# The sample chunk of the delta rule, with four heads stacked on 128 partitions

## The reference, cut to what matters

```python
def step(s, xs):                      # one chunk; s is (values, keys) per head
    u = w_v_c - einsum('bhtk,bhvk->bhtv', w_k_c, s)
    o = einsum('bhtk,bhvk->bhtv', q_dec_c, s) + einsum('bhts,bhsv->bhtv', p_c, u)
    s = gl[..., None, None] * s + einsum('bhtv,bhtk->bhvk', u, k_dec_c)
    return s, o
```

## Time and profile before

| | us |
|---|---|
| runs | 2828.75, 2826.97, 2824.72 |
| median | 2826.97 |
| profiled execution | 2828.19 |
| its span, first to last instruction | 2826.6 |
| TensorE busy (share) | 2722.1 (96%) |
| VectorE busy | 1281.5 (45%) |
| ScalarE busy | 858.5 (30%) |
| GpSimd busy | 408.3 (14%) |
| mean granted TensorE clock | 0.970 |

### The profile page before, as it was taken

How to read it: one execution, slowest core, us unless ns; L and a number is a source line. 1 busy time by engine, 2 the same in 40 slices (tenths; PEclk the granted TensorE clock), 3 DMA queues, 4 the chain that set the end, 5 groups by cost and what they waited for, 6 DMA issues and landing times.

```text
span 2826.6 us, 52279 instructions
## 1 busy us (share of the span) xinstructions
PE 2722.1 (96%) x20734; PEld 2547.0 (90%) x20734; DVE 1281.5 (45%) x2130; ACT 858.5 (30%) x1429; POOL 408.3 (14%) x577
## 2 busy tenths in 40 slices
PE   7999999999888999999999999899999899999998
PEld 6999998876445899999899999899999868999998
DVE  5444227455443544432544432676445544544423
ACT  3222223234332422222422222443323223322222
POOL 3000003001442100000100000554244220100001
PEclk9999999999999999999999999999899958999999
DMA  3323322223996233332232332233101023223331
GB/s 115 89 84 92 99 75 76 61 69 112 352 341 200 60 89 89 87 104 78 60 89 83 91 103 74 58 90 82 35 1 31 9 67 98 74 83 89 99 92 43
DMA packets 404839, 263.03 MB, mean 93 GB/s; under 512 B 10954, under 2 KB 378775, under 8 KB 404665
## 3 DMA queue, kind: packets, MB, share of 16 engines
q1 hardware_dynamic: 394332, 227.22, 27.4%
q0 software_dynamic: 10384, 34.09, 3.5%
HBM read 251.71 MB, written 9.56 MB: 92 GB/s over the span
## 4 chain that ended last, share of the span: by engine, by line
PE 90%; DVE 5%; issue 1%; ACT 1%; POOL 1%; DMA 1%; SPq 0%; DVEq 0%; POOLq 0%; ACTq 0%
PE ps L484 66%; PE ps L470 5%; PE ps L2205 2%; PE ps L2226 1%; PE ps L1361 1%; PE ps L2223 1%; PE ps L1373 1%; PE ps L1413 1%; PE ps L498 1%; PE ps L1304 1%; PE ps L1322 1%; PE ps L2335 1%; PE ps L2314 1%; PE ps L1305 1%; PE ps L2189 1%
## 5 line engine op out<-in xcount | busy, mean ns | idle before, releaser
L462 DVE TENSOR_TENSOR w_lo<-w_raw,w_hi 128x1024 fp32r<-128x1024 f32 (+1 forms) x314 | 419.0, 1335 | 964.9 <-ACT w_hi L455 963.6
L484 PE MATMUL ps<-hd_hi,w_hi 128*128 128x272 f32 x3728 | 777.9, 290 | 4.0 <-DVE w_lo L462 4.0
L484 PE MATMUL ps<-hd_lo,w_hi 128*128 128x272 f32 x3728 | 771.4, 288 | 0.0
L484 PE MATMUL ps<-hd_hi,w_lo 128*128 128x272 f32 x3728 | 769.4, 288 | 0.0
L455 ACT CAST w_hi<-w_raw 128x1024 fp32r<-128x1024 f32 (+1 forms) x314 | 350.7, 1117 | 1092.9 <-PE ps L484 1031.3
L484 PEld LDWEIGHTS ps<-hd_hi,w_hi 128*128 128x128 f32 x3728 | 585.3, 189 | 12.1 <-issue 11.7
L484 PEld LDWEIGHTS ps<-hd_lo,w_hi 128*128 128x128 f32 x3728 | 587.8, 189 | 0.0
L484 PEld LDWEIGHTS ps<-hd_hi,w_lo 128*128 128x128 f32 x3728 | 584.7, 189 | 0.0
L959 POOL TENSOR_TENSOR xT<-xT,rstd_rows 128x272 f32<-128x272 f32 x96 | 81.8, 879 | 1778.5 <-DVE rstd_rows L984 1778.5
L484 PE MATMUL ps<-h_hi,w_hi 128*128 128x272 f32 x1232 | 255.0, 288 | 0.0
L484 PE MATMUL ps<-h_lo,w_hi 128*128 128x272 f32 x1232 | 254.5, 288 | 0.0
(11 more groups left out here) (493 smaller groups left out, 3230.8 us busy)
## 6 DMA issues: line engine op xcount, KB each, us to landing
w_raw<-in_ffn_w_gate_dram SPq DMA_DIRECT2D x88, 512.0 KB, 3.9
w_raw<-in_ffn_w_up_dram SPq DMA_DIRECT2D x88, 512.0 KB, 3.8
w_raw<-in_ffn_w_down_dram SPq DMA_DIRECT2D x64, 704.0 KB, 4.5
k_pages<-in_cache_a_k_dram SPq DMA_DIRECT2D x128, 256.0 KB, 4.5
v_pages<-in_cache_a_v_dram POOLq DMA_DIRECT2D x128, 256.0 KB, 4.5
w_raw<-in_c_w_in_dram SPq DMA_DIRECT2D x33, 512.0 KB, 4.1
w_raw<-in_ab_w_in_dram SPq DMA_DIRECT2D x25, 512.0 KB, 4.0
w_raw<-in_ab_w_out_dram SPq DMA_DIRECT2D x8, 512.0 KB, 3.8
```

The lines of the kernel that those rows point to most:

```text
L462: e.tensor_tensor(w_lo[:, n % 2, 0:nk * P], raw[:, n % RAW, 0:nk * P], w_hi[:, n % 2, 0:nk * P].bitcast(F32), ALU.subtract).then_inc(sem(" ...
L484: mm = e.matmul(ps[:, bank + h, 0:TH], w, x[:, k0 + k, half(h)], start=first and k == 0 and w is wh and x is x_hi, stop=last and k == nk - ...
```

## The change

The sample chunk now treats the four heads of a group as one block: 4 heads x 32 tokens = 128 partitions. Masks, decays, norms, the triangular system, right side, updates and outputs are one 128x128 tile per group where there were four 32x32 or 32x128 ones, and `incl_s`, `same_s` have 128 rows.

Products by the states are turned around. The turned states are the moving operand (128 columns), and the stationary operand is a copy of the keys or queries of one head (32 columns) that has only the tokens of sample b, all others zero. Each head writes its own 32 PSUM partitions (column groups), and the eight samples add up in one bank. GpSimd makes the masked copies in prompt chunk 3, behind the masks of levels 2 to 5. States are turned by sample, four heads into one bank, in 16 units; ScalarE copies out 12 of them, VectorE 4.

State changes are four sets (group, half of the samples) of four products with 32 rows, each head on its own rows of the array (row groups) and into its own bank. Set 0 stands between the halves of the first `c_out` unit, sets 1 to 3 ahead of units 1 to 3; VectorE's additions go between its weight splits. GpSimd masks the keys (two instructions) and issues the stores of the states.

```diff
+        def samples_masked(gp, y):                              # pool_delta
+                to = kq_m[gp][y]
+                mark(e, "pool_small", e.memset(to[:, :, :], 0.0))
...
+                e.tensor_copy(to[:, :, 0:252].rearrange("p j (b x) -> p j b x", x=36)[:, :, :, 0:DEC_S], src[:, :, 0:7, :])
+                ins = e.tensor_copy(to[:, :, 252:256], src[:, :, 7, :])
...
                     if l == 2:
                         masked_gates(c + 1)
+                    if 2 <= l < 6 and c == PT - 1:
+                        for y in range(2):
+                            samples_masked((l - 2) // 2, 2 * (l % 2) + y)
...
+            def keys_by_states(u):                              # pe_delta
...
                 for j in range(GH):
+                    mm = e.matmul(ps[j * NS:(j + 1) * NS, 4 * gp + 2, 0:P], kq_m[gp][j // 2][:, j % 2, b * NS:(b + 1) * NS],
+                                  s_turned[:, u % 8, j, :], start=b == 0, stop=b == DEC_B - 1)
...
+            def state_changes(n):
...
+                for j in range(GH):
+                    at = slice(j * NS, (j + 1) * NS)
+                    mm = e.matmul(ps[:, 4 + j, :], tile("u_vec", PT, gp)[at, 0, :],
+                                  kd_m[gp][at, 4 * q:4 * q + 4, :].rearrange("p b k -> p (b k)"), start=True, stop=True)
                 mm.then_inc(sem("ds_psum"), 1)
...
+            for u in range(2, 8):                               # TensorE's order
+                states_turned_in(u)
+                keys_by_states(u - 2)
+                if u == 3:
+                    both(corrections, PT, 1)
+                if u == 5:
+                    both(output_turned, PT - 1)
+            for u in (6, 7):
+                states_turned_in(u + 2)
+                keys_by_states(u)
+            for u in range(8):
+                queries_by_states(u)
+            for u in range(10, 16):
+                states_turned_in(u)
+                keys_by_states(u - 2)
+                if u == 10:
+                    updates(PT, 0)
+                if u == 12:
+                    outputs_within(PT, 0)
+            for u in (14, 15):
+                keys_by_states(u)
+            for u in range(8, 16):
+                queries_by_states(u)
+            updates(PT, 1)
+            outputs_within(PT, 1)
+            out_opening()                                       # unit 0 of c_out, first half of the tokens
+            state_changes(0)
             both(output_turned, PT)
...
+            outputs_out(PT, 0)                                  # VectorE's order
+            dve_split(e, gemms["c_out"]["n0"], 0, KD)
+            e.wait_ge(sem("final_state"), 2)
+            prompt_low(0)
+            prompt_low(1)
+            state_out(13)
+            for k in range(2, 5):
+                prompt_low(k)
+            right_side(PT, 1)
+            prompt_low(5)
+            outputs_out(PT, 1)
+            prompt_low(6)
+            prompt_low(7)
+            outputs_normed(PT)
+            gated(PT)
...
+            new_states(0)
```

More of the change, by code:

```diff
@@ L737, in whole @@
                     e.wait_ge(sem("y_squared"), i * per + (y_base[g["name"]] + t - 1))
[L738 to L740 removed]
+                if g["name"] == "c_out" and isinstance(i, int) and i == 0:
+                    if j == 0:
+                        e.wait_ge(sem("mixed_parts"), KD + 1)
+                        for k in range(KD):
+                            mm = pe_passes(e, n, k, x_hi, x_lo, k, 0, 1, k == 0, k == KD - 1)
+                        mm.then_inc(sem("unit_done"), 1)
+                        return
+                    state_changes(j)
                 pe_unit(e, n, i, g["nk"], x_hi, x_lo, (j % 2) * KU if per == 2 else 0, 2 * (t % 2),
[L742 to L743 removed]
+                        opens, per == 4 or j % 2 == 1)
             for j in range(4):
@@ L2182, in key_rows @@
                 e.wait_ge(sem("e_ready"), turn_of(c, gp))
-                for j in range(GH):
+                for j in range(heads(c)):
                     mm = e.transpose(bank(3, c, gp)(j), of_chunk(1, c)(gp, j), ident[:, :])
@@ L2187, in by_keys @@
             def by_keys(x, to, c, gp):
-                for j in range(GH):
-                    mm = e.matmul(bank(to, c, gp, n_of(c))(j), of_chunk(1, c)(gp, j), of_chunk(x, c)(gp, j), start=True, stop=True)
+                for j in range(heads(c)):
+                    mm = e.matmul(bank(to, c, gp)(j), of_chunk(1, c)(gp, j), of_chunk(x, c)(gp, j), start=True, stop=True)
                 mm.then_inc(sem("kk_psum"), 1)
@@ L2193, in x0 @@
                 e.wait_ge(sem("xt1_ready"), turn_of(c, gp))
-                for j in range(GH):
-                    mm = e.transpose(bank(1, c, gp, n_of(c))(j), tile("x_t", c, gp)[:, j, :], ident_of(c))
+                for j in range(heads(c)):
+                    mm = e.transpose(bank(1, c, gp)(j), tile("x_t", c, gp)[:, j, :], ident[:, :])
                 mm.then_inc(sem("x0_psum"), 1)
@@ L2339, in pe_delta, with out_opening @@
+            def out_opening():
+                g = gemms["c_out"]
+                e.wait_ge(sem("w_lo_ready"), g["first"] + 1)
+                for k in range(KD):
+                    e.wait_ge(sem("mixed_parts"), k + 1)
+                    pe_passes(e, g["first"], k, hd_hi, hd_lo, k, 0, 0, k == 0, k == KD - 1)
             both = lambda f, *args: [f(*args, gp) for gp in range(2)]
@@ L2392, in pe_delta @@
             states_turned_in(0)
+            states_turned_in(1)
             for gp in range(2):
@@ L2440, in pe_c @@
                 e.transpose(ps[:, 0, c * P:(c + 1) * P], ba_t[:, c * P:(c + 1) * P], ident[:, :])
-            e.transpose(ps[0:NS, 1, 0:P], ba_t[:, SEQ:T], ident[:, :]).then_inc(sem("tensor_stage"), reached("ba_psum"))
+            for j in range(GH):
+                mm = e.matmul(ps[j * NS:(j + 1) * NS, 1, 0:P], ba_t[:, SEQ:T], ident[:, :], start=True, stop=True)
+            mm.then_inc(sem("tensor_stage"), reached("ba_psum"))
             e.wait_ge(sem("conv_acc"), PRIMED + 24)
@@ new lines, in outputs_normed @@
+                own, n = slice(head_cols(c, 0).start, head_cols(c, 1).stop), 2 * heads(c)
+                total, root, tmp, fac = (t[:, 0:n] for t in (o_sum, o_rs, o_tmp, o_fac))
+                chain(e, e.tensor_tensor(total, total, q_sq[:, own], ALU.mult))
+                chain(e, e.tensor_scalar(total, total, EPS, None, ALU.add))
+                dve_rsqrt(e, root, tmp, total)
+                chain(e, e.tensor_tensor(fac, root, r_q[:, own], ALU.mult))
+                for gp in range(2):
+                    e.tensor_tensor(tile("o", c, gp), tile("o", c, gp), of_heads(fac[:, gp * heads(c):(gp + 1) * heads(c)], P),
```

572 lines of the change are left out of this document (265 added, 307 removed).

## The result

In the first comparison the changed kernel took **2784.6 us** (2782.4 to 2786.8, 4 runs), the kernel before 2827.0 (4 runs): ratio 0.9843 [0.9831, 0.9855], 42 us less. Predicted were 2793 us, 34 less, with a forecast range of 2781 to 2806. A second comparison on another occasion gave 2787.6 and 2827.6: 0.9855 [0.984, 0.987], 40 less. The profiled execution of after has a span of 2785.2 us, that of before 2826.6.

The account below looks back on a forecast made before the run. TensorE's list was taken to bound the kernel: 45 us gained before c_out, less 7.4 paid back, less 4.5 in chunk 3, plus 1.0, gave 34 us and 2793 us. Forecast range 2781 to 2806, whole range 2775 to 2813.

Parts of the forecast that it names:

- 1, products by the states: Before c_out: 32 sets of four key or query products, 0.35 us a set, 11.2 us at full clock.
- 2, transposes: Before c_out: 64 state transposes, eight in 0.93 us at full clock, 7.4 us instead of 13.6.
- 1 to 3 together: TensorE's products by states, transposes and small 128-partition products before c_out: 22.9 us at full clock.
- 4 and 5, waits and clock: Before c_out: waits of 12 us (6 to 18), and 8 us (0 to 22.9) for work at half speed.
- (b): TensorE's wait for the outputs of the last prompt chunk, while GpSimd scales states: 2.97 us becomes 4.6.
- (c): TensorE can't turn unit 15 until VectorE copies unit 13, behind a weight split and two low parts: 4.4 us.
- 6, state changes among units: Among c_out units: a set of four row-group products takes 1.0 us; with waits 7.4 us paid back (3.7 to 18).
- Rival B: Little gained: row groups run in turn (+10.8), clock stays 0.50 up to c_out (+15); 8 us, 2819; chance 0.11.
- 7, GpSimd in chunk 3: GpSimd's masked copies in chunk 3 hold up VectorE's norm chain, TensorE waits: 4.5 us lost (0 to 6).
- 8, smaller edits: Fewer chunk 3 transposes and square sums gain 1.0 us; constants done during the projection and moved stores cost nothing.
- A: More gained: clock holds, copy of unit 13 in time, GpSimd run leaves chain alone; 51 us, 2776; chance 0.10.
- C: Slower: with 128 columns the column groups don't overlap, 32 sets 58 us, not 11; 2840; chance 0.04 shared with another rival.

Follow-up runs that it names:

- columns_serial: Changed kernel with all four heads' products of keys and queries by the states on one group of 32 output columns: 2801.3 us.
- experiment 4: The changed kernel again, 2787.6 us, and beside it four_edits, 2772.1 us; the wait of 0.56 us is from four_edits.
- the repeat: The changed kernel measured once more, unaltered, as the base of a later batch: 2787.6 us.
- rows_serial: Changed kernel with all four products of a set of state changes reading partitions 0 to 31, one row group: 2793.2 us.
- copies_later: Changed kernel with GpSimd's masked copies between the masks of levels 3 to 6 of chunk 3, not 2 to 5: 2787.4 us.
- six_edits: four_edits plus VectorE copying state unit 5 ahead of chunk 3's gate and GpSimd's last four state scalings behind the eight low parts of c_out: 2773.4 us.
- four_edits: Changed kernel with masks built behind the c_qkv units, masked copies after the sample gates' scaling, unit 13 and right side earlier, state scaling after the norm chain: 2772.1 us.
- unit13_first: Changed kernel with VectorE's copy of state unit 13 ahead of the first weight split of c_out, not behind it and two low parts: 2785.2 us.

## Why the prediction was right, and where it was off

The mechanism was right: TensorE's list was what the end waited for, and it gave 53 us where I said 45, paid back 5.4 where I said 7.4. That the total came near also has luck in it: the miss in chunk 3 (+3) and the one in the constants (-3) cancel, and neither was foreseen. By its steps:

*1, products by the states: right.* 0.35 and 0.23 a set against 0.35; 9.3 us at full clock against 11.2. columns_serial shows that this rests on the four groups.

*2, transposes: 15% low.* Four turns between two column sets take 0.53 to 0.59 (2259.48 to 2260.07), not 0.46: about 9 us instead of 7.4. The Trainium skill, page "TensorEngine Tiling (Array Packing)", section "Key Properties", says that a change of tiling mode drains the engine; the extra 0.07 to 0.13 us per alternation is of that kind, and no run here isolates it.

*1 to 3 together: right.* 35.0 less the idles (3.27 + 0.30 + 3.08 + 0.46 = 7.1) and less half speed (5.9 x 0.49 + 6.7 x 0.38 = 5.4) leaves 22.5; I said 22.9.

*4 and 5, waits and clock: places right, sizes too large.* 7.1 against 12 and 5.4 against 8. (a) 0.30, not 2: the copies keep up. (b) 3.27, not 4.6. (c) 3.08, not 4.4. (d) 0.46, not 1. In (b) the chain stood beside GpSimd's scalings for four steps, as I had it (0.53 to 0.98 us each), and with no scaling beside it the wait was 0.56 (experiment 4). These 7.5 us are most of the surplus before c_out. That the clock came back because the work is dense in columns was argued and isn't tested: behind the same 3.27 us it stayed at half speed for 5.5 us in the trace after and for some 3.5 in the repeat.

*6, state changes among units: right.* A set takes 1.07 (1.0 forecast; the estimate of 1.2 beside it was too high), and rows_serial shows 3.7 without row groups. The waits are 0.45, 1.47 and 0.34. What I left out: c_out now opens at full clock, where before its opening ran at 0.50, and that gave some 2.7 back. Without this term the payback would be 8.1, and my 7.4 would have been a little low, not 2 too high. (Rival B's +10.8 for four sets at 3.6 instead of 1.0 should read +10.4; nothing else hangs on it.)

*7, GpSimd in chunk 3: the term that was mis-sized.* 1.5 us lost (18.12 against 16.60 from level 1 to the outputs), not 4.5. VectorE in the trace after:
```profile
2213.72 1.13 DVE L2874 TENSOR_SCALAR norms<-norms 128x8 f32<-128x8 f32 x1
2214.89 1.65 DVE L882 TENSOR_SCALAR norms<-norms 128x8 int32<-128x8 int32 x1
...
2217.82 1.27 DVE L887 SCALAR_TENSOR_TENSOR norms<-norms 128x8 f32<-128x8 f32 x1
2219.12 1.19 DVE L885 TENSOR_TENSOR norms<-norms 128x8 f32<-128x8 f32 x1
2220.34 0.17 DVE L886 SCALAR_TENSOR_TENSOR norms<-norms 128x8 f32<-128x8 f32 x1
```
GpSimd:
```profile
2213.56 2.49 POOL L2128 TENSOR_TENSOR mt<-u,half_masks 128x512 f32<-128x512 f32 x2
2215.99 0.52 POOL L2113 MEMSET qk_masked<- 128x512 f32 x1
...
2217.81 2.48 POOL L2128 TENSOR_TENSOR mt<-u,half_masks 128x512 f32<-128x512 f32 x2
...
2303.94 3.62 POOL L2158 DMA_DIRECT2D out_dram<-states  x4 [17.85 <-DVE states L2934]
...
2319.53 3.52 POOL L2158 DMA_DIRECT2D out_dram<-states  x4 [11.97 <-DVE states L2934]
```
As in the earlier trace rows, the chain stands still beside the masks, here four times, while six steps of 0.17 to 0.20 pass between 2216.58 and 2217.79 beside a memset and small copies. I let the copies close the run; they left it open. But not for every step: the TENSOR_SCALAR of 1.65 us, longer than one mask, ends at 2216.54, and the masks at 2216.05; what ends at 2216.51 is the memset. With the two of copies_later, all three TENSOR_SCALAR steps that met a memset in these two traces waited for its end; the TENSOR_TENSOR and SCALAR_TENSOR_TENSOR steps passed. The Trainium skill, page "SBUF — State Buffer", section "Who interferes with whom", has a VectorE instruction with two SBUF inputs contend with a GpSimd instruction only where that one reads SBUF, and the loser wait for the whole of one instruction: the last two waits above agree (1.27 and 1.19 us, each for one mask of 1.24), the 3.24 us of the earlier trace rows do not.

*8, smaller edits: one wrong.* The constants were not "done during the projection": they stand ahead of its first unit, VectorE's first step there waits for them, and their growth cost 2.2 us, 2.9 with what else differs up to the staging. I judged them by when their values are read; I should have read the chain of the kernel before at 1802 to 1817, where each of them has its row. The stores were hidden, as forecast: 3.62 and 3.52 us for four issues each (2303.94 and 2319.53 above), and GpSimd is wanted later.

Sum of the misses against the forecast 34: stage +8, payback +2, chunk 3 +3, constants -3, and 1.4 in two parts that the change leaves alone (0.8 ahead of chunk 3, 0.6 at the end); less the 4.3 that this execution lost in shared code: 41, as the ledger has it.

Of the rivals, A named three places where less was lost than forecast, but in none of them was the loss nothing: the chain cost 1.5 us, unit 13 3.08, and the clock fell twice. B is ruled out by rows_serial and the clock of 1.00 between the waits, C by columns_serial, D by the stores' rows and E by the ledger.

## What to carry to other kernels

Four small products on four column or row groups cost little more than one (0.23 us against 0.89 for four in a row, 1.07 against 3.70), so cut TensorE's list first; then the gain sits in waits of 3 us behind small VectorE chains, and each edit that shortens one shows the next (unit 13, then the right side; the low parts, then the sample's chain). Put GpSimd's work on SBUF where VectorE has no chain that TensorE waits for: moves alone, nothing removed, took the time from 2787.6 to 2768.3, in two batches. And ask of every "constant" which semaphore it stands ahead of, not when it is read.

## What the hardware showed unexpectedly

- VectorE steps of 0.16 us took 0.96 to 1.05 beside GpSimd's scalings in six_edits, one step for each. Three of the four were TENSOR_SCALAR with one SBUF input and 2 columns, so not only operations on two inputs wait; and such steps waited for memsets too (0.43 and 0.67 us in copies_later, the end of 1.65 in the trace after).
- Idle time and clock are not one to one: after 1.94 and 0.46 us of idle in four_edits the clock fell to half (eight products at 0.43 us), after 2.10 and 0.46 in unit13_first it held (0.29), and after 2.11 in columns_serial it was at half some 1.1 us after the work began again. What decides between them is open.
